# Weights loaded in units of 512 columns into a ring of two buffers, in place of units of 256 columns into a ring of four

## The reference, cut to what matters

```python
for l in range(DEPTH):                      # 2
    h = rmsnorm(x, norm1_g[l])
    z = h @ w_in[l]                         # 1024 -> 2824 columns: q, k, v, forget, gu, gv, c_in, c_b, c_c
    ...                                     # attention, gated MLP, gated convolution, their norms
    x = x + mixed @ w_out[l]                # 1024 -> 1024
    h2 = rmsnorm(x, norm2_g[l])
    x = x + peer_ffn(h2, w_query[l], sub_keys[l], expert_u[l], expert_v[l])

def peer_ffn(...):
    q = (ht @ w_query)                      # 1024 -> 2048, 8 heads x 2 halves x 128
    # scores against 128 sub-keys per half, top 16 of each half, top 16 of the 256 pairs -> e_idx, gate
    a = jnp.einsum('chkd,cd->chk', expert_u[ec], xc)
    w = jax.nn.gelu(a) * gc
    return jnp.einsum('chk,chkd->cd', w, expert_v[ec])
```

## Time and profile before

| | us |
|---|---|
| median of three runs | 3128.44 |
| lowest and highest of the three | 3126.62 and 3134.91 |
| the profiled execution's own time | 3116.28 |
| its span, first to last instruction | 3114.5 |
| PE busy | 2423.6 (78%) |
| DVE busy | 1980.4 (64%) |
| ACT busy | 1268.6 (41%) |
| POOL busy | 1222.6 (39%) |

### The profile page before, as it was taken

The page is one execution under the profiler, slowest core; times in us unless marked ns, Lnnn a source line. Parts: engine busy times, 40 slices in busy tenths (PEclk is TensorE's granted clock), DMA queues, the critical chain, the costliest instruction groups (busy, mean ns, idle before and its releaser), DMA issues.

```text
span 3114.5 us, 39018 instructions
## 1 busy us (share of the span) xinstructions
PE 2423.6 (78%) x13088; PEld 1040.1 (33%) x13088; DVE 1980.4 (64%) x4707; ACT 1268.6 (41%) x3741; POOL 1222.6 (39%) x1064
## 2 busy tenths in 40 slices
PE   6678877998895788878697698888888566656675
PEld 6545344643461343223252244223344111111110
DVE  1465655667637766778546775787745777777654
ACT  1133633367333433753333433674333333333333
POOL 0133433333334433444333343335434455445553
PEclk9789888998896898678697799788799666666666
DMA  7499999999999999999999999999999999999997
GB/s 244 167 407 388 412 404 360 377 401 357 362 369 382 400 409 407 420 372 415 385 407 409 369 411 406 414 394 393 410 388 389 395 422 421 421 380 422 421 421 330
DMA packets 277809, 1203.90 MB, mean 387 GB/s; under 512 B 26600, under 2 KB 144872, under 8 KB 146536
## 3 DMA queue, kind: packets, MB, share of 16 engines
q0 software_dynamic: 147456, 1073.81, 84.4%
q1 hardware_dynamic: 130152, 127.60, 12.5%
HBM read 1199.24 MB, written 2.10 MB: 386 GB/s over the span
## 4 chain that ended last, share of the span: by engine, by line
DMA 40%; PE 36%; DVE 7%; ACT 7%; issue 6%; POOL 2%; another core or an unknown queue 1%; SPq 0%; POOLq 0%; DVEq 0%; ACTq 0%
DMA arena<-in_uv,eidx 37%; PE bank L1029 20%; PE acc L1217 15%; DVE arena L1015 4%; POOL arena L534 2%; DMA unit<-in_w_in 1%; ACT L701 1%; ACT diag L710 1%; ACT wts L704 1%; ACT L626 1%; ACT gelu L701 1%; DMA unit<-in_w_query 1%; PE heads L1029 1%; ACT region L626 1%
## 5 line engine op out<-in xcount | busy, mean ns | idle before, releaser
L534 POOL DMA_INDIRECT arena<-in_uv,eidx x1024 | 1193.9, 1166 | 1731.4 <-PE acc L1217 1488.5
L1015 DVE CUSTOM_DVE_ANT_0 arena<-arena,h_nat 128x1024 f32<-128x1024 f32 x1024 | 1255.4, 1226 | 931.1 <-DMA arena<-in_uv,eidx 919.3
L1217 PE MATMUL acc<-arena,diag 64*64 64x512 f32 x8192 | 1398.3, 771 | 471.3 <-ACT diag L710 389.4
L701 ACT ACTIVATE gelu<-dots 128x1 f32<-128x1 f32 x1024 | 207.0, 202 | 1523.8 <-DVE dots L1015 1507.0
L1217 PEld LDWEIGHTS acc<-arena,diag 64*64 64x64 f32 x8192 | 258.4, 155 | 1207.8 <-ACT diag L710 933.4
L1029 PE MATMUL bank<-hT,unit 128*128 128x256 f32 (+1 forms) x2400 | 506.1, 359 | 65.8 <-DMA unit<-in_w_in 22.8
L1029 PEld LDWEIGHTS bank<-hT,unit 128*128 128x128 f32 x2400 | 385.4, 199 | 296.9 <-issue 235.3
L710 ACT ACTIVATE diag<-identc,wts 128x64 f32<-128x64 f32 x1024 | 356.0, 348 | 33.6
L704 ACT ACTIVATE wts<-gelu,gate 128x1 f32<-128x1 f32 x1024 | 301.7, 295 | 33.3
L1029 PE MATMUL bank<-unit,hT 128*128 128x256 f32 x896 | 228.0, 397 | 10.3 <-issue 5.0
L1029 PEld LDWEIGHTS bank<-unit,hT 128*128 128x128 f32 x896 | 164.5, 193 | 116.1 <-issue 88.8
(11 more groups left out here) (127 smaller groups left out, 1323.2 us busy)
## 6 DMA issues: line engine op xcount, KB each, us to landing
unit<-in_w_in SPq DMA_DIRECT2D x55, 1024.0 KB
unit<-in_w_query SPq DMA_DIRECT2D x40, 1024.0 KB
unit<-in_w_out SPq DMA_DIRECT2D x20, 1024.0 KB
arena<-in_uv,eidx POOLq DMA_INDIRECT x1024
x<-in_x SPq DMA_DIRECT2D x4, 512.0 KB, 8.7
out<-hT SPq DMA_DIRECT2D x4, 512.0 KB, 5.4
gain<-in_norm_g SPq DMA_DIRECT2D x2, 512.0 KB, 12.0
wsp<-in_w_spatial SPq DMA_DIRECT2D x2, 256.0 KB
```

The lines of the kernel that those rows point to most:

```text
L534: nc.gpsimd.indirect_dma_start(arena[:, n % NBUF, :], None, uv, bass.IndirectOffsetOnAxis(ap=eidx[:, seq % 2, j:j + 1], axis=0)).then_inc( ...
L701: nc.scalar.activation(gelu[:, group], dots[:, group], ACT.Gelu_apprx_tanh).then_inc(s_ge, GROUP)
L1015: V.tensor_tensor_reduce(out=uu, in0=uu, in1=h_nat[:, seq % 3, :], scale=1.0, scalar=0.0, op0=ALU.mult, op1=ALU.add, accum_out=dots[:, n % ...
L1217: ins = nc.tensor.matmul(acc[rows][cols * HALF:(cols + 1) * HALF, :], diag[own, n % NBUF, :], arena[own, n % NBUF, D + f * 512:D + (f + 1) ...
```

## The change

Weights now go in units of 512 columns, two of the old ones side by side, through a ring of two buffers. CC stays alone, 256 columns wide, since CI and CB lie ahead of it in `w_in` and are needed after it. A pass has 12 loads in place of 23: G, CC, CI+CB, V, Q, K, O01, O23, QY01, QY23, QY45, QY67. Eleven of them are 2 MB in 1024 pieces of 2 KB, one is 1 MB in pieces of 1 KB. The ring holds the same 4 MB. SP waits ahead of a load until the last product of the unit two before it is complete. PE's products, their order and everything on DVE, ACT and POOL stay as they were.

```diff
-UNITBUF = 4
+UNITBUF = 2
+UNIT = 512
...
-    units = list(IN) + [("O", f) for f in range(N_OUT)] + [("QY", c) for c in range(NQ)]
+
+    units = [("in", O_G, UNIT, (("G", 0), ("G", 1))), ("in", O_C + 2 * CW, CW, (("CC", 0),)),
+             ("in", O_C, 2 * CW, (("CI", 0), ("CB", 0))), ("in", O_V, UNIT, (("V", 0), ("V", 1))),
+             ("in", O_Q, UNIT, (("Q", 0), ("Q", 1))), ("in", O_K, UNIT, (("K", 0), ("K", 1)))]
+    units += [("out", f * COLS, UNIT, (("O", f), ("O", f + 1))) for f in range(0, N_OUT, 2)]
+    units += [("query", c * COLS, UNIT, (("QY", c), ("QY", c + 1))) for c in range(0, NQ, 2)]
+    unit_of = {key: (n, k) for n, u in enumerate(units) for k, key in enumerate(u[3])}
...
-        wring = [sb(f"unit{n}", [P, DC, COLS]) for n in range(UNITBUF)]
+        wring = [sb(f"unit{n}", [P, DC, UNIT]) for n in range(UNITBUF)]
...
-        def unit_no(p, *key):
-            return p * NU + units.index(key)
-
         def wait_unit(eng, p, *key):
-            n = unit_no(p, *key)
+            k, part_of = unit_of[key]
+            n = p * NU + k
             eng.wait_ge(s_unit[n % UNITBUF], 16 * (n // UNITBUF + 1))
-            return wring[n % UNITBUF]
-
-
-        def last_reader(p, n):
-            name, f = units[n]
+            return wring[n % UNITBUF][:, :, part_of * COLS:(part_of + 1) * COLS]
+
+
+        def last_reader(p, k):
+            name, f = units[k][3][-1]
             return (p, list(OUT_PARTS)[-1], f) if name == "O" else (p, name, f)
...
-            def load_unit(p, name, f):
-                l, n = passes[p][0], unit_no(p, name, f)
+            weights = {"in": w_in, "out": w_out, "query": w_query}
+
+            def load_unit(p, k):
+                n = p * NU + k
                 if n >= UNITBUF:
 
                     m = turn(*last_reader((n - UNITBUF) // NU, (n - UNITBUF) % NU))
                     sp.wait_ge(full[m % RING], m // RING + 1)
...
-                sp.dma_start(wring[n % UNITBUF][:], src).then_inc(s_unit[n % UNITBUF], 16)
+                matrix, o, width, _ = units[k]
+                sp.dma_start(wring[n % UNITBUF][:, :, 0:width],
+                             weights[matrix][passes[p][0], :, :, o:o + width]).then_inc(s_unit[n % UNITBUF], 16)
...
-                for k, (name, f) in enumerate(units):
-                    load_unit(p, name, f)
+                for k in range(NU):
+                    load_unit(p, k)
                     if k == UNITBUF - 1:
                         if opens_layer(p):
                             load_layer(p)
```

More of the change, by code:

```diff
@@ L355, in wait_freed @@
             eng.wait_ge(free[n % RING], n // RING + 1)
-        def unit_no(p, *key):
-            return p * NU + units.index(key)
         def wait_unit(eng, p, *key):
-            n = unit_no(p, *key)
+            k, part_of = unit_of[key]
+            n = p * NU + k
             eng.wait_ge(s_unit[n % UNITBUF], 16 * (n // UNITBUF + 1))
-            return wring[n % UNITBUF]
-        def last_reader(p, n):
-            name, f = units[n]
+            return wring[n % UNITBUF][:, :, part_of * COLS:(part_of + 1) * COLS]
+        def last_reader(p, k):
+            name, f = units[k][3][-1]
             return (p, list(OUT_PARTS)[-1], f) if name == "O" else (p, name, f)
-        roots_of_pass = 4
         squares_before = [4 * first_seq[p] for p in range(NP + 1)]
```

## The result

| | before | changed |
|---|---|---|
| median of four runs, us | 3128.14 | 3178.30 |
| lowest and highest | 3126.62, 3134.91 | 3165.66, 3181.01 |
| profiled execution, us | 3116.28 | 3176.16 |
| its span | 3114.5 | 3174.4 |

The changed kernel is slower: 1.0167 times the time before, 95% interval 1.0146 to 1.0188, or 50 us. The forecast was 3117, its range 3100 to 3139. The two profiled executions lie 59.9 us apart. That is what the traces have to explain, and about 10 us of it is the spread of single executions: the profiled one of before was the fastest of its four, 12 us under the median. Of all executions behind this document one, of wide_where_slack, fell in a slow state (3763.29 us at a granted clock of 0.542) and is left out of its ratio.

A forecast was written before the change was run, and what follows sets the result against it. The prediction took the DMA engines, at 96.9% of their time, as the bound except where PE is. Its terms, -20 + 3 + 3 + 0 + 1 + 2 = -11 us on the median of 3128.4, gave 3117, 80% range 3100 to 3139.

The forecast's parts named there:

- The packet's price: DMA engines: a 2 KB packet costs 0.085 us, two of 1 KB 0.095; saves 0.63 us per 2 MB unit.
- 31.5 x 0.63 us = 20 us under full DMA: Passes 0 to 4: 31.5 wide units count as under full DMA, each saving 0.63 us, together 20 us.
- So 2 MB takes 10.3 us, and with some 2 us of latency (my guess) 12: Pass 1: load time at 0.24 gathers per weight packet; PE waits 6 us at CI+CB, 2 each at Q and K.
- +3, +3 and +1: Net added PE waits: 3 us in pass 1, 3 at CI+CB of pass 2, 1 at QY45 of pass 1.
- as the chain shows: 22.9 and 21.7: Full DMA: 1 MB computed at 21 us beside gathers, with two chain rows of 22.9 and 21.7 us as support.
- The slower rival: CI+CB of passes 1 and 2 takes 23.4 us, PE waits 17 and 13: +12, 3140 us; mark over 12; chance 0.15.
- "0" for passes 3 and 4: CI+CB there: PE waits 10 us, but up to eight gathers keep DMA busy through it, so 0 us cost.
- The check written down beforehand: From 320 to 2400 us: prediction wrong if DMA share falls by more than the packets do, time lost to emptied queues.
- Q and QY45 of pass 1: Weight loads in pass 1: PE waits 2 us at Q and 1 us at QY45.
- The opening: Before the first slot: `keysT` lands 3.0 us earlier, PE waits 4 us at CI+CB and 1 at Q; net +2.
- The rival of the packet size: SP's queue: packet size doesn't matter, same DMA share in half the packets, only waits stay; 3137 us, chance 0.12.
- The large gain: Full DMA: 2 KB packets go at the gather's price, faster weights remove most waits; -30 us, 3098, chance 0.13.

The follow-up runs named there:

- wide_where_slack: Changed kernel with 512-column loads only where the load has time, all others 256 columns in the order of before; 3130.62 us, 1.0017 to before.
- extra_2k: own_halves plus 28 MB of unread weights after the last real loads, in 2 KB pieces beside gathers; 3191.06 us, 1.0218 to before.
- own_halves: Changed kernel with every 256-column half a load of its own (1 KB pieces), asked for and awaited alone; 3124.65 us, 1.0002 to before.
- pair_1k: Changed kernel with each 512-column unit brought by two 256-column DMAs (1 KB pieces), asked for and awaited together; 3223.81 us, 1.0316 to before.
- extra_1k: own_halves plus 28 MB of unread weights after the last real loads, in 1 KB pieces beside gathers; 3192.22 us, 1.0222 to before.

## Why the prediction was wrong, step by step

**The packet's price: right.** 0.0852 us against 0.085, 72,952 packets, 356 us of SP's packets against 354, and with gathers alone (2600 to 2700 us) still 421 GB/s. The Trainium skill's line rate at 512 B and more (DMA: Bandwidth & Descriptors, section Specifications) would have made both sizes equal per KB; these runs show 0.0473 against 0.0426, so the measurement decides against it.

**"31.5 x 0.63 us = 20 us under full DMA": the size of this term failed.** The work did fall by 25 us of all engines. It is time only if DMA never stands empty, and before it nearly never did (a share of 1.00 in layer 0). In the changed kernel the saving came back as empty DMA. With CI+CB by halves, layer 1 gave 6 of its 13 us; in extra_2k, where PE waits for none of the extra loads, 3.4 of 8.5 showed.

**"So 2 MB takes 10.3 us, and with some 2 us of latency (my guess) 12": the step that failed first.** It sized the waits of PE in passes 1 and 2, and through them +3, +3 and +1, where layer 0 lost 46.5. A load's time was worked out as 1024 packets at the mean mix of a stretch. All DMA packets from the first packet of CI+CB until PE went on, in pass 1, pass 2 and pass 3:

```profile
DMA packets 1657, 4.87 MB, mean 387 GB/s; under 512 B 64, under 2 KB 64, under 8 KB 1395
...
DMA packets 1896, 6.29 MB, mean 406 GB/s; under 512 B 80, under 2 KB 80, under 8 KB 1478
...
DMA packets 2350, 9.76 MB, mean 410 GB/s; under 512 B 129, under 2 KB 129, under 8 KB 1504
```

That is 262 gathers to 1331 weight packets, 418 to 1398 and 846 to 1375: 0.20, 0.30 and 0.62, where 0.24, 0.38 and 0.90 were taken. So at CI+CB the mix was not too low. Two other things were missing. First, from the issue to the first weight packet 3.4, 3.9 and 3.9 us passed, in which gathers went on alone (173 packets in pass 1); it was 1.3 us in the opening, where there are none. The forecast had a guess of 2 us in pass 1 and nothing in passes 2 to 4. Second, not 1024 but 1331 to 1398 weight packets went by until the load had landed on all 16 engines and PE went on. They can only be those of V, which SP asks for when CC is used up (270.4 us in pass 1): its load is under way on the engines before the one ahead of it counts as landed. With both, the forecast's own prices come out: 3.4 + (262 x 0.3113 + 1331 x 0.085) / 16 = 15.6 us against 16.0, then 19.5 against 19.4 and 27.7 against 27.7. At Q and QY45 of pass 1 the mix failed as well: 516 gathers to 1357 weight packets and 541 to 1321 are 0.38 and 0.41, beside the 0.24 of the stretch.

Nor do the rows of the chain give a load's time, as the prediction took them to ("as the chain shows: 22.9 and 21.7"). During the 22.9 us of before, 2683 weight packets of 1 KB went by, 2.6 loads and not one, at 0.29 gathers to a packet and not 0.90:

```profile
DMA packets 3588, 9.06 MB, mean 395 GB/s; under 512 B 136, under 2 KB 2819, under 8 KB 2819
```

That 1024 packets at 0.90 also give 21 us is luck. The slower rival leaned on the same row.

**"0" for passes 3 and 4: wrong in its place.** The gathers cover the wait, and are then used up. What they don't cover is the time after it, and no term had that. The check written down beforehand was the one that hit: the DMA share from 320 to 2400 us fell from 0.99 to 0.97, some 50 us, and SP's packets were only 23 us less of it.

**Q and QY45 of pass 1: mis-sized**, 9.6 and 9.2 us against 2 and 1. These loads are the 21.1 and 21.8 us of the chain. own_halves has the wait at Q too, and not the one at QY45.

**The wait alone was priced, and not PE's clock behind it.** No term had it; in layer 0 it is at most the 12 us by which PE's busy time grew.

**The opening: +7.7 against +2.** SP issued `keysT` at 12.27 us, earlier than the 15.94 of before, and PE came to CI 2.4 us earlier than before. It then waited 5.0 us at CI+CB against 4, and its 64 records there took 9.83 us, where 64 of the same kind at 62 us took 7.41: 2.4 more, behind the wait. At Q and K it waited 1.2 and 0.5 against 1. That makes 6.7 of the 7.7. own_halves, with the same order but half loads, starts its first slot at 149.4 us, so it is the wide loads that cost it.

**The slower rival had the right place and the wrong price.** It set CI+CB of passes 1 and 2 as the place, and some 30 of the 50 us go with CI+CB of all passes. It was to decide from 18 us from issue to landing, and in pass 2 that load took 19.4. But its own mark, a wait over 12 us, was never reached in passes 1 and 2 (10.0 and 8.9), and it came to 3140: it had no term for Q, QY45, the clock or layer 1's lost gain, and counted a wait once, as idle PE, and not the queue that is empty behind it. The rival of the packet size fell with pair_1k and the extra loads. The large gain fell as well: it rested on the faster weights, and in extra_2k these are what leaves a hole open.

Open: how much of the 50 us is PE at half clock (at most 12 in layer 0; only tried at CI+CB), which loads beside CI+CB hold the rest of the loss, and why wide_where_slack lost time in layer 0. That holes take the gain in the dense passes too is argued from the extra loads, not shown.

## What to carry to other kernels

Less work for a full engine is less time only as long as its queue never runs dry: look at what keeps the queue filled (here PE, by freeing arena buffers) before pricing the saving. A wait can cost more than its own length if the work that refills a queue stands behind it, and can cost nothing elsewhere: 60.8 us of waits in own_halves were free, 82.4 in the changed kernel went with a loss of 50. Compare stretches between the same instructions, not at the same times, once one kernel is late. Take the time of a load from loads that are alone in their queue at that place, with the time to the first packet and the loads that follow, and not from a row that spans several or from 1024 packets at a mean mix; and weigh a larger unit against the time between its asking and its need.

## What the runs showed of the hardware

Two queues that both have work share the DMA engines by packets, not by bytes: 0.90 gather packets of 8 KB passed for each weight packet, whether it had 1 KB or 2 KB (2500 to 2600 us of extra_1k and extra_2k). So a load beside a full queue of gathers goes by its number of packets. In extra_1k nine steps from one issue to the next, 2598.3 to 2786.4 us, took 20.9 us each for 1 MB in pieces of 1 KB; in extra_2k five steps, 2514.0 to 2632.2 us, took 23.6 us each for 2 MB in pieces of 2 KB. Both are what turn-taking gives (21 and 23.4 us in the prediction), and the second is 1.8 times as fast per byte at only 10% less work. While CI+CB of passes 1 and 2 loaded in the changed kernel the ratio was lower (0.20 and 0.30), and the load took less time.

Beside gathers, 3.4 to 3.9 us passed from a load's issue to its first packet; without them, in the opening, 1.3 us.
